# Expert down weights loaded by column range, in a decoder step on one Trainium2 core

## The reference

```python
def hmoe(xn, r_group, r_expert, w_gu, w_down):
    ...                                     # top-1 group, top-2 experts inside it
    comb = jnp.sum(jax.nn.one_hot(eid, N_EXPERTS) * wts[..., None], axis=1)
    y = jnp.zeros((n, D), jnp.float32)
    for e in range(N_EXPERTS):
        gu = x2 @ w_gu[e]                   # 1024 -> 1024
        hdn = jax.nn.silu(gu[:, :D_EXPERT]) * gu[:, D_EXPERT:]
        y = y + comb[:, e:e + 1] * (hdn @ w_down[e]).astype(jnp.float32)   # 512 -> 1024
    return y.astype(xn.dtype).reshape(B, T, D)
```

## Time and profile before

| | us |
|---|---|
| median of 3 executions (1125.61, 1127.4, 1130.25) | 1127.4 |
| the profiled execution | 1125.39 |
| its span, first to last instruction | 1123.6 |
| PE busy in the span | 982.4 |
| DVE, ACT busy | 340.3, 265.9 |
| weights of the experts of both layers | 2 x 96 units of 1 MiB |
| first gate and up matmul, last down matmul, layer 0 | 97.0, ends 320.4 |
| the same, layer 1 | 878.2, ends 1104.7 |

### The profile page before, as it was taken

The page is one execution under the profiler, slowest core; times in us unless marked ns, Lnnn a source line. Parts: engine busy times, 40 slices in busy tenths (PEclk is TensorE's granted clock), DMA queues, the critical chain, the costliest instruction groups (busy, mean ns, idle before and its releaser), DMA issues. The chain is left out here.

```text
span 1123.6 us, 14758 instructions
## 1 busy us (share of the span) xinstructions
PE 982.4 (87%) x5628; PEld 566.4 (50%) x5629; DVE 340.3 (30%) x963; ACT 265.9 (24%) x585; POOL 29.2 (3%) x81
## 2 busy tenths in 40 slices
PE   2959999999947998599999996889977999999994
PEld 2745343333323443598888874656536433333331
DVE  1263222222222037403333334156626122212221
ACT  2022111111120103113444443046512211111110
POOL 0010000000000000300000000000001000000000
PEclk9968999999987999679999997579995999999997
DMA  9924999999949151786476633300017999999992
GB/s 324 376 69 171 396 409 409 409 409 409 409 152 352 71 224 74 147 289 199 139 226 202 188 122 106 148 3 1 2 27 301 410 408 408 409 409 408 409 409 106
DMA packets 97945, 284.86 MB, mean 254 GB/s; under 512 B 16256, under 2 KB 21504, under 8 KB 97351
## 3 DMA queue, kind: packets, MB, share of 16 engines
q1 hardware_dynamic: 97871, 283.86, 67.7%
HBM read 277.61 MB, written 14.71 MB: 260 GB/s over the span
## 5 line engine op out<-in xcount | busy, mean ns | idle before, releaser
L785 PE MATMUL bank<-weight_ring,moe_gatheredT 128*64 128x512 f32 x1024 | 226.1, 594 | 1.1 <-DMA weight_ring<-in_w_gate_up 1.1
L785 PEld LDWEIGHTS bank<-weight_ring,moe_gatheredT 128*64 128x64 f32 x1024 | 72.2, 137 | 145.1 <-issue 140.9
L822 PE MATMUL bank<-weight_ring,moe_hiddenT 128*64 128x512 f32 x512 | 114.1, 596 | 14.3 <-ACT moe_hiddenT L881 8.6
L1538 PE MATMUL bank<-arena_b 128*128 128x256 f32 x512 | 120.9, 387 | 0.0
L1538 PEld LDWEIGHTS bank<-arena_b 128*128 128x128 f32 x512 | 95.4, 193 | 13.3 <-issue 1.2
L822 PEld LDWEIGHTS bank<-weight_ring,moe_hiddenT 128*64 128x64 f32 x512 | 36.1, 137 | 81.9 <-issue 67.4
L926 DVE TENSOR_TENSOR moe_hidden<-moe_silu,bank 128x256 f32<-128x256 f32 x32 | 13.5, 421 | 197.4 <-ACT moe_silu L875 197.4
L938 DVE SCALAR_TENSOR_TENSOR moe_down_parts<-bank,moe_slot_weight,moe_down_parts 128x512 fp32r<-128x512 f32 x32 | 22.6, 747 | 163.9 <-ACT moe_down_parts L893 163.9
L875 ACT ACTIVATE moe_silu<-bank 128x256 f32<-128x256 f32 x32 | 12.3, 384 | 243.6 <-PE bank L785 243.6
L840 PE MATMUL bank<-moe_down_parts,moe_scatter 128*128 128x512 f32 (+1 forms) x192 | 56.8, 429 | 4.5 <-DVE moe_down_parts L938 4.5
L947 DVE TENSOR_TENSOR residual<-bank,residual 128x512 f32<-128x512 f32 (+1 forms) x96 | 59.0, 678 | 2.3 <-PE bank L840 2.3
(11 more groups left out here) (302 smaller groups left out, 1107.5 us busy)
## 6 DMA issues: line engine op xcount, KB each, us to landing
weight_ring<-in_w_gate_up SPq DMA_DIRECT2D x128, 1024.0 KB, 17.0
weight_ring<-in_w_down SPq DMA_DIRECT2D x64, 1024.0 KB, 16.1
arena_b<-in_pages_raw SPq DMA_DIRECT2D x64, 256.0 KB, 3.0
arena_b<-in_pages_sel SPq DMA_DIRECT2D x64, 256.0 KB, 3.9
out_new_win_sample<-in_state_win SPq DMA_DIRECT2D x1, 8064.0 KB
arena_b<-in_w_kv SPq DMA_DIRECT2D x3, 2048.0 KB, 15.5
arena_b<-in_win_keysT SPq DMA_DIRECT2D x8, 512.0 KB, 5.0
arena_b<-in_state_win SPq DMA_DIRECT2D x8, 512.0 KB, 5.8
```

The lines of the kernel that those rows point to most:

```text
L785: last = pe.matmul(ps[e % 2][g * CAP:(g + 1) * CAP, :], XS[:, b % 2, k, x * CAP:(x + 1) * CAP], w[:, :, g, :], start=(k == 0), stop=(k == ...
L822: last = pe.matmul(ps[3 + half][x * CAP:(x + 1) * CAP, :], HT[:, x, c % 2, (c // 2) * CAP:(c // 2 + 1) * CAP], RW[:, (n + x) % RING, c % 2 ...
L1538: last = pe.matmul(at, W1[:, kind, half, i, :], rhs, start=(half + i == 0), stop=(half + i == 8), skip_group_check=True)
```

## The change

A down unit now holds all 512 rows of one expert but only half of the columns. `load_unit` reads, for units 8 and 9 of a pair, columns 0 to 511 of the two experts, and for units 10 and 11 columns 512 to 1023. The slot and its size stay. `down(p)` runs over the half first: it waits for units 8 and 9, does all four row blocks of bank 3, waits for units 10 and 11, and does bank 4. ACT's `down_high` waits for each half apart, and scatter and adds take the three row tiles of half 0 first, then those of half 1.

```diff
 def load_unit(sp, I, M, layer, n):
     pair, j = divmod(n, UNITS)
     if j < KD:
-        e, at, src = 2 * pair + j // 4, 2 * P * (j % 4), I["w_gate_up"]
+        e, at = 2 * pair + j // 4, 2 * P * (j % 4)
+        dst, src = M["ring"][:, n % RING], I["w_gate_up"][layer][e, at:at + 2 * P, :].rearrange("(a p) n -> p a n", p=P)
     else:
-        e, at, src = 2 * pair + j % 2, 2 * P * ((j - KD) // 2), I["w_down"]
-    sp.dma_start(M["ring"][:, n % RING], src[layer][e, at:at + 2 * P, :].rearrange("(a p) n -> p a n", p=P))\
-        .then_inc(M["unit_in"][n % RING], 16)
+        e, half = 2 * pair + j % 2, (j - KD) // 2
+        dst = down_unit(M, n)
+        src = I["w_down"][layer][e, :, half * 512:(half + 1) * 512].rearrange("(a p) n -> p a n", p=P)
+    sp.dma_start(dst, src).then_inc(M["unit_in"][n % RING], 16)
+
+def down_unit(M, n):
+    return M["ring"][:, n % RING].rearrange("p a (b n) -> p (a b) n", b=2)
...
             def down(p):
                 pe.wait_ge(ht, 2 * p + 2)
                 reach(pe, yl, 2 * p)
-                for c in range(NF):
-                    n = UNITS * p + KD + 2 * (c // 2)
-                    if c % 2 == 0:
-                        pe.wait_ge(unit_in[n % RING], landings(n))
-                        pe.wait_ge(unit_in[(n + 1) % RING], landings(n + 1))
-                    for half in range(2):
+                for half in range(2):
+                    n = UNITS * p + KD + 2 * half
+                    pe.wait_ge(unit_in[n % RING], landings(n))
+                    pe.wait_ge(unit_in[(n + 1) % RING], landings(n + 1))
+                    for c in range(NF):
                         for x in range(2):
                             last = pe.matmul(ps[3 + half][x * CAP:(x + 1) * CAP, :],
...
             def scatter(p):
-                pe.wait_ge(yl, 2 * p + 2)
...
-                for t, rows in enumerate(TILE_ROWS):
-                    for half in range(2):
-                        m = 2 * t + half
+                for half in range(2):
+                    pe.wait_ge(yl, 2 * p + half + 1)
+                    for t, rows in enumerate(TILE_ROWS):
+                        m = NT * half + t
...
             def down_high(p):
-                act.wait_ge(used, UNITS * (p + 1))
                 act.wait_ge(ws, 2 * p + 2)
                 reach(act, scattered, NM * p)
                 for half in range(2):
+                    act.wait_ge(used, UNITS * p + KD + 2 * half + 2)
```

More of the change, by code:

```diff
@@ L814, in down @@
                 reach(pe, yl, 2 * p)
-                for c in range(NF):
-                    n = UNITS * p + KD + 2 * (c // 2)
-                    if c % 2 == 0:
-                        pe.wait_ge(unit_in[n % RING], landings(n))
-                        pe.wait_ge(unit_in[(n + 1) % RING], landings(n + 1))
-                    for half in range(2):
+                for half in range(2):
[3 more added lines that the diff above has]
+                    for c in range(NF):
                         for x in range(2):
                             last = pe.matmul(ps[3 + half][x * CAP:(x + 1) * CAP, :],
-                                             HT[:, x, c % 2, (c // 2) * CAP:(c // 2 + 1) * CAP],
-                                             RW[:, (n + x) % RING, c % 2, half * 512:(half + 1) * 512],
+                                             HT[:, x, c % 2, (c // 2) * CAP:(c // 2 + 1) * CAP], down_unit(M, n + x)[:, c, :],
                                              start=(c == 0), stop=(c == NF - 1))
-                            if half == 1 and c % 2:
+                            if c == NF - 1:
                                 last.then_inc(used, 1)
             def scatter(p):
-                pe.wait_ge(yl, 2 * p + 2)
                 pe.wait_ge(st_ready, p + 1)
```

## The result

The changed kernel has a median of 1132.02 us (1131.51 to 1132.71, five executions) against 1125.61 us for the kernel before in the same rounds (1124.05 to 1130.25). The ratio on record is 1.0043, with a 95% interval of 1.0023 to 1.0064: slower, by a little under the 0.5% that I called no change. It is an estimate from all executions of both kernels and not the quotient of the two medians, which is 1.0057. The forecast was 1132, +0.4%.

What follows compares the result with a forecast made beforehand. The weight stream's rate bounds both expert stages, with a tail behind each last landing. Profiled 1125.39 + 8.4 (stream) - 4.0 (tails) = 1129.8 us; on the median 1131.8, rounded to 1132, range 1126 to 1137.

Steps and rivals of the forecast that it cites:

- The bound: Both expert stages: each ends by the last unit's landing, set by the weight stream's rate, plus a tail behind it.
- The price of a unit: Weight stream: a down unit in 2 KiB rows takes 2.70 us instead of 2.56, +0.14 us.
- (b): Weight stream: short rows cost more, +0.20 us a unit, giving 1135.4 us, +0.7%; chance 0.26.
- The upper bound of 0.20: Weight stream: most a down unit's 2 KiB rows should add, in us, reckoned from the packets' own time.
- The number of units: Down units loaded while the stream is the bound: 28 in layer 0 (+3.9 us), 32 in layer 1 (+4.5 us).
- The tails: Work behind each layer's last landing: 8.80 us after the change, gaining 1.5 us in layer 0, 2.5 in layer 1.
- (a): Weight stream: short rows cost half the forecast price or nothing, 1127.6 or 1123.4 us; chance 0.13.
- (c): PE's granted clock drops to 1.2 GHz before the last landing; for one layer 1136.1 us; chance 0.06.
- (d): Tails: half 0 added early after all, up to 1.4 us more gain each, about 1129 us; chance 0.04.

Runs made afterwards that it cites:

- load-only run: Changed kernel with ACT's waits, scatter and adds as in the kernel before; column-range load and down matmul order kept: 1132.81 us against 1125.48, ratio 1.0072.
- kernel by blocks: Kernel before, 4 KiB rows kept; behind each landing half 0's four matmuls precede half 1's, parts, scatter and adds go by half: ratio 0.9967 (0.9944 to 0.9989).

## Why the prediction was right

**The bound.** It is the stream. With pieces of 2 KiB the end moves out, with pieces of 8 KiB it moves in until PE is the bound.

**The price of a unit.** I took 0.14 us from the rates of the earlier trace rows; between landings a down unit takes 2.71 us instead of 2.56, so it is 0.15. The 402 GB/s that I named came out as 401. My sign for (b), windows under 400, was badly set: the 0.16 us at which (b) begins would also show as 401, so the windows cannot tell the two apart, and the landings can. The upper bound of 0.20, from the packets' own time, was too high: packets overlap, and not equally (102.3% and 104.4% of 16 engines in the earlier trace rows).

**The number of units.** From the first gate and up matmul to the start of the last eight, layer 0 takes 222.95 us instead of 219.75 (+3.2, forecast +3.9), and layer 1 227.80 instead of 222.83 (+5.0, forecast +4.5). Together it is +8.2 us against +8.4. The load-only run, with the same load, has +4.0 in layer 0 (96.43 to 320.15) and +4.8 in layer 1 (880.67 to 1108.29), which 28 and 32 units at 0.15 us fit (4.2 and 4.8); single executions differ by up to 0.8 us.

**The tails.** I had 8.80 us, and both are 8.75. The gains are 1.6 and 2.6 us against 1.5 and 2.5. One part of the second was read wrongly: I took the slow scatter of layer 1 for a result of PE's idle 2.23 us and so for something that the change removes. The load-only run has the same idle time and no slow scatter. One us of the 4.2 belongs to that execution of the kernel before, and a fair count for the change is 3.2.

**The number itself.** That the median lies within 0.1 us of 1132 is luck. I had built on 1127.4 for the kernel before, and in these rounds it ran at 1125.61. The change of +4.4 us that I forecast compares with 6.4 between these medians, 4.8 by the ratio and 4.0 in the stages. What holds are the terms: +8.2 against +8.4 for the stream, -4.2 against -4.0 for the tails.

**The rivals.** (a) fell with the load-only run. By the Trainium skill ("DMA: Bandwidth & Descriptors", section "Why small descriptors are slow (HBM only)"), with some 3 cycles of overhead for each packet, the estimate was 2.3% for a halved piece; the trace disagrees, with 6% (2.71 against 2.56 us). (b) needed more than 0.16 us a unit, so it was near, but the distance in memory on which it rested in part costs nothing. (c) did occur in layer 1 and was hidden: the granted clock was 0.69 on average while PE worked at the last pair's first eight matmuls,

```profile
1100.00:1104.70 4.70, 3.08 (x18) 1.48 (x14) 0.73 (x3) 1.53 (x4) 0.00 (x0) 1.00 1.05 387
1104.70:1110.10 5.40, 5.26 (x16) 1.59 (x16) 0.00 (x0) 0.00 (x0) 0.00 (x0) 0.69 0.75 278
1110.10:1113.80 3.70, 3.65 (x17) 1.33 (x17) 0.75 (x1) 0.69 (x1) 0.00 (x0) 1.00 0.00 0
```

and they took 5.26 us instead of 3.65. Nothing was lost, though by little. The last unit was issued at 1095.92 and landed 14.1 us later, at 1110.02. The second eight start at 1110.15, 0.13 us behind that landing; the first eight started as long behind theirs (1104.67, 1104.81). They had ended at 1110.07, so one more matmul at that clock would have been on the path. My argument against (c) looked at the wrong stretch. The clock had fallen by the time these eight began, and what stands before them is the end of the last gate and up, transposes and waits, in which PE was busy 3.08 of 4.70 us. In layer 0 the first eight took 3.65 us after the same work, so what decides it stays open. Of (d) there is no sign: DVE's adds come in one piece behind the last `down_low`.

**The chances.** The ratio lies 0.07% under my line between no change and slower, and its interval reaches over it. Giving the two 0.50 and 0.46 was as much as the numbers could say.

## What to carry to other kernels

Where a stage is bound by its weight stream, count the pieces of a transfer and not only its bytes: here each piece cost some 9 ns of an engine's time beside its bytes, from 1 KiB to 8 KiB. Before a load is cut differently to let later work begin early, see if the order of the compute alone does it; here the kernel by blocks got the whole gain from the order of matmuls, scatter and adds, with its rows left whole. And where a few us are in question, compare the stages in the traces, since the whole times carry the spread of other stages.

## What the runs showed that I had not expected

- A unit of 1 MiB takes 3.01, 2.71, 2.56 and 2.49 us between landings in pieces of 1, 2, 4 and 8 KiB, with 387, 401, 409 and 419 GB/s in the windows (at 1 and 2 KiB only every third unit has the short pieces). The 9 ns for each piece that I had worked out between 2 and 4 KiB hold on both sides of them.
- A matmul on 64 columns of the array costs 0.9 us alone and 0.9 us beside one on the other 64 columns.
- SP's issue of a down unit went from 941 to 2371 ns in median, and the landing of gate and up units came 15.4 us after their issue instead of 17.0 on the page. That fits a queue that holds fewer bytes when they come in shorter pieces; no run tests it. SP's slower issue is not the price of the short rows: the DMA engines are as full as before (a share of 1.03 in the windows), and at the end units still land some 14 us or more after their issue and 2.56 or 2.71 us apart, so the queue did not run dry.
- The granted clock fell during layer 1's last pair though PE's longest wait there was 1.72 us. In layer 0 it stayed at 1.00 with the same wait.
